# Differential attention: sums of squares by two fp32r passes over a rounded part and a remainder

## Chip, cores and metric

The kernel runs on one core of one Trainium2 chip. The metric is the device time of one execution, in microseconds (us); the time given is the median of three runs.

## What is computed

Two transformer blocks of two layers each over 512 tokens of width 1024. The change lies in the last mixer, differential attention with 8 heads. Cut to what matters:

```python
def rms_norm(x, g):
    return x * lax.rsqrt(jnp.mean(x * x, axis=-1, keepdims=True) + NORM_EPS) * g

k = rms_norm(k.reshape(B, S, 8, 2, 64), k_norm)                 # keys: means over 64 columns
q = rms_norm((xn @ w_q).reshape(B, S, 8, 2, 64), q_gain) * 64 ** -0.5
s = q @ k, causal; p = softmax(s)
a = p[:, :, 0] - lam * p[:, :, 1]                               # two maps per head
o = a @ v                                                       # (S, 128) per head
o = rms_norm(o, head_gain) * (1.0 - lambda_init)                # means over 128 columns
return o.reshape(B, S, 8 * 128) @ w_out
```

So each head needs three sums of squares: of its queries, of its keys and of its output.

## The kernel before

Everything is held transposed, features on the 128 partitions and the 512 tokens along the row (P = 128, TOK = 512). A sum over features is therefore a sum over partitions, and TensorE does it: a matmul with `ones` (all 128 partitions) or `blockones` (two blocks of 64) as its weights.

Large products use fp32r, a form of fp32 of which TensorE reads a rounded value. To keep the precision each operand is split in a high part (an ACT copy that writes fp32r) and a low part (a DVE subtraction, value minus high part), and `mm3` adds three matmuls: high with high, high with low, low with high. Weights come by DMA in chunks of 128 x 2048 into three slots in turn (`raw_w`); `round_weights` makes `high_w` on ACT and `split_weights` makes `low_w` on DVE. The sums of squares, the scores, the transposes and the product with the values are plain fp32 matmuls.

The program is written out by hand, one instruction stream for each engine, each in a fixed order; semaphores alone connect them. Differential attention runs from about 1762 us to 1942 us of the span. `attention_steps` calls `project` for head 0, then `step(p, st, nx, prev)` for p = 0 to 7, then `tail`. In step p the scores of head p are made, while TensorE also computes queries and keys of the next head (`nx`, p + 1), turns the probabilities of the head before (`prev`) and multiplies them by its values, and sums the squares of the output of head p - 2 (`head_sum`). Step 7 has no next head; there the first chunks of the output projection (`resid_first`, `resid_pe`) take that place.

For queries (which = 0) and keys (which = 1) the path is: `half` twice on TensorE (24 matmuls into bank `which`), `raw` on DVE (times `rstd`, into `f_raw`, which is the tile xf), `square` on ACT (into `sq[:, which, :]`), `sums` on TensorE (back into bank `which`), `root` on ACT (Ln, then Exp, into `sq[:, 2 + which, :]`), `normed` on DVE. The next head's `half` may write the bank once Ln has read it (semaphore `logged`). For a head's output: `output` and `output_square` on ACT, `head_sum`, `head_root` on ACT, `head_scale` on DVE, then `rounded` (ACT) and `split` (DVE) for the output projection.

The order on DVE near the end of a step matters to what follows: `norm(p, st)`, `normed(nx, 0)`, `raw(nx, 1)`, `split_weights`, `normed(nx, 1)`. The weights that this `split_weights` finishes are those of the first `half` of the next step. On ACT it is `root(nx, 0)`, `place_values`, `copy_pt`, `round_weights`, `square(nx, 1)`, `output`, `root(nx, 1)`, `output_square`.

Of the kernel before, what the change touches and what calls it, by code (L numbers as in the profile page):

```python
# [31 lines left out]
P = 128  # L32
# [91 lines left out]
def _build(nc, dram, ctx):  # L124
# [43 lines left out]
    def sb(name, shape, dt=F32):  # L168
        return ctx.enter_context(nc.sbuf_tensor(name, shape, dt))

    def sem(name):
        return ctx.enter_context(nc.semaphore(name))
# [4 lines left out]
    sq = sb("sq", [P, 4, TOK])  # L177
# [4 lines left out]
    ones = sb("ones", [P, P])  # L182
    blockones = sb("blockones", [P, P])
    eps = sb("eps", [P, 1])
# [4 lines left out]
    def area(name, specs, start):  # L189

        at, out = start, []
        for n, shape, dt in specs:
            size = int(np.prod(shape[1:])) * 4
            out.append(nc.alloc_sbuf_tensor_at(f"{name}_{n}", list(shape), dt, offset=at))
            at += (size + 63) // 64 * 64
        assert at <= nc.sbuf_usable_end, (name, at, nc.sbuf_usable_end)
        return out, at


    wh, lows = area("high", [(f"w{i}", (P, SLOT), F32R) for i in range(NS)], ring_base)  # L200
# [44 lines left out]
    (f_kh, f_kl, f_vo, f_q0, f_q1, f_k0, f_k1, f_v, f_p, f_pt, f_causal), _ = area("diff", [  # L245
# [3 lines left out]
        ("causal", (P, TOK), F32)], arena_base)  # L249
# [39 lines left out]
    consts_made = sem("consts_made")  # L289
    out_stored = sem("out_stored")  # L290
# [11 lines left out]
    def stand_alone(ins):  # L302


        return ins.wait_op(consts_made, 2, "sem-ge")

# [1583 lines left out]
    F = sems("diff", "v_staged v_placed q_made raw_staged squared sums_made logged rooted q_staged k_staged "  # L1890
             "scored masked exped inverted p_scaled normed turned pt_copied pv_done o_taken")
    H = sems("hn", "squared summed logged rooted scaled rounded split")
# [69 lines left out]
    def diff_pe(pe):  # L1962
# [19 lines left out]
        def sums(p, which):  # L1982

            pe.wait_ge(F["squared"], 2 * p + which + 1)
            pe.wait_ge(F["raw_staged"], 2 * p + which + 1)
            pe.matmul(ps[:, which, :], blockones[:, :], sq[:, which, :], start=True, stop=True)\  # L1986
              .then_inc(F["sums_made"], 1)
# [36 lines left out]
        def head_sum(p):  # L2024

            pe.wait_ge(F["o_taken"], p + 1)
            pe.wait_ge(H["squared"], p + 1)
            pe.matmul(ps[:, O_BANK, :], ones[:, :], sq[:, 0, :], start=True, stop=True)\
              .then_inc(H["summed"], 1)

# [56 lines left out]
    def diff_act(act):  # L2087
        def square(p, which):
            act.wait_ge(F["raw_staged"], 2 * p + which + 1)
            wait_past(act, F["sums_made"], 2 * p - 1 + which)  # L2090
            if which == 0:
                wait_past(act, H["summed"], p - 2)
            act.activation(sq[:, which, :], f_raw[:, which, :], ACT.Square).then_inc(F["squared"], 1)

# [39 lines left out]
        def output_square(p):  # L2134
            act.wait_ge(F["sums_made"], clip(2 * p + 5, 2 * NHD))
            wait_past(act, H["summed"], p)
            act.activation(sq[:, 0, :], ps[:, O_BANK, :], ACT.Square).then_inc(H["squared"], 1)

# [65 lines left out]

        diff_values_act(act, 0)
# [5 lines left out]
    def diff_dve(dve):  # L2211
        def raw(p, which):
            if which == 0:
                dve.wait_ge(F["q_made"], p + 1)
            else:
                dve.wait_ge(w_used, st_diff.base + p + 1)
            wait_past(dve, F["k_staged" if which else "q_staged"], p)
            wait_past(dve, F["squared"], 2 * p - 1 + which)
            dve.tensor_tensor(f_raw[:, which, :], ps[:, which, :], rstd[:, :], ALU.mult)\
               .then_inc(F["raw_staged"], 1)  # L2220

# [50 lines left out]
        def step(p, st, nx, prev):  # L2272
            mask(p, st, (0, 1))
            if nx:
                raw(nx[0], 0)
            else:
                split(2)
            mask(p, st, (2, 3))
            if past_two(p):
                head_scale(p - 2)  # L2280
            if not nx:
                split(3)
            norm(p, st)
            if nx:
                normed(nx[0], nx[1], 0)
                raw(nx[0], 1)
            else:
                split(4)
            if p == NHD - 2:
                split(0, 1)  # L2290
            split_weights(dve, st_diff.base + p + 2)
            if nx:
                normed(nx[0], nx[1], 1)

        def tail(p, st):
            split(5)
            head_scale(p - 1)
            split(6)
            split_weights(dve, st_bout.base + 2)
            head_scale(p)  # L2300
            split(7)

        def project(p, st):
            for which in range(2):
                raw(p, which)
            for which in range(2):
                normed(p, st, which)
# [85 lines left out]
    def _(pe):  # L2393
        pe.wait_ge(consts_made, 2)
        for _ in range(16):
            pe.matmul(ps[:, O_BANK, 0:P], ones[:, :], ones[:, :], start=True, stop=True)
        latents_pe(pe)
# [23 lines left out]
    def _(act):  # L2421
        act.wait_ge(consts_made, 2)
        log_exp(act)
        input_act(act, f_attn0)
# [214 lines left out]
```

## Time and profile before

| | |
|---|---|
| median of three runs | 2322.74 us (2322.34 to 2325.74) |
| profiled execution | span 2323.5 us, first to last instruction; the page gives no other time of it |
| PE (TensorE matmul) busy | 2297.7 us, 99% |
| PEld (weight loads) busy | 1862.3 us, 80% |
| DVE busy | 1115.8 us, 48% |
| ACT busy | 882.1 us, 38% |
| share of PE in the chain that ended last | 94% |
| mean granted TensorE clock | 0.998 of full speed |

The chain that ended last is followed back from the last instruction to what released each step. Where PE has 94% of it, time is PE's own work nearly everywhere, and another engine counts only where PE stood idle for it. A matmul's busy time overlaps the next one's, so what one costs in a row of matmuls is the distance from its start to the next start, not its duration.

### The profile page before, as it was taken

How to read it: one execution, taken by the hardware profiler on the slowest of the kernel's cores; microseconds unless marked ns; L12 is line 12 of the kernel's file. 1: busy time of each engine (PE TensorE's matmuls, PEld its weight loads, DVE VectorE, ACT ScalarE, POOL GpSimd, SP SyncE). 2: the span in 40 equal slices, each digit the busy share in tenths (PEclk: the TensorE clock that was granted, in tenths of full speed). 3: DMA queues.
4: the chain of work that ended last, by engine and by line, in shares of the span. 5: the costliest groups of instructions: out<-in, count | busy, mean ns of one | idle time of the engine just before them, and what ended most of it. 6: DMA issues, size and time to landing. Idle time of an engine off the chain costs nothing.

```text
span 2323.5 us, 26379 instructions
## 1 busy us (share of the span) xinstructions
PE 2297.7 (99%) x10880; PEld 1862.3 (80%) x10880; DVE 1115.8 (48%) x1723; ACT 882.1 (38%) x1399; POOL 0.2 (0%) x4
## 2 busy tenths in 40 slices
PE   9999999999999999999999899999999999999999
PEld 7777888888778888888888788888886667888887
DVE  5655443444575443445577554334444565432432
ACT  5654321223474322224434443223344675421321
POOL 0000000000000000000000000000000000000000
PEclk9999999999999999999999999999999999999999
DMA  3222222322222223223211132322322111222222
GB/s 142 80 82 73 91 98 93 109 85 88 86 97 73 92 91 111 97 80 102 96 64 55 55 109 92 108 91 94 106 98 73 55 55 70 94 91 102 98 91 91
DMA packets 36582, 206.51 MB, mean 89 GB/s; under 512 B 4192, under 2 KB 5088, under 8 KB 17136
## 3 DMA queue, kind: packets, MB, share of 16 engines
q1 hardware_dynamic: 34128, 199.43, 24.9%
q10 hardware_dynamic: 2336, 5.41, 0.7%
q8 instruction: 86, 1.41, 0.3%
q14 instruction: 32, 0.26, 0.0%
HBM read 202.73 MB, written 2.10 MB: 88 GB/s over the span
## 4 chain that ended last, share of the span: by engine, by line
PE 94%; ACT 2%; DVE 2%; issue 1%; ACTq 0%; DVEq 0%
PE ps L309 29%; PE ps L311 28%; PE ps L310 28%; PE ps L1062 2%; PE ps L1649 1%; DVE low_w L335 1%; PE ps L2001 1%; PE ps L1115 1%; PE ps L1086 1%; PE ps L1110 1%; PE ps L1078 0%; ACT high_w L327 0%; PE ps L1674 0%; PE ps L572 0%; PE ps L1986 0%
## 5 line engine op out<-in xcount | busy, mean ns | idle before, releaser
L309 PE MATMUL ps<-xh,high_w 128*128 128x512 f32 x1584 | 628.7, 397 | 0.0
L311 PE MATMUL ps<-xh,low_w 128*128 128x512 f32 x1584 | 617.4, 390 | 0.0
L310 PE MATMUL ps<-xl,high_w 128*128 128x512 f32 x1584 | 616.8, 389 | 0.0
L335 DVE TENSOR_TENSOR low_w<-raw_w,high_w 128x2048 fp32r<-128x2048 f32 (+3 forms) x208 | 422.9, 2034 | 188.2 <-ACT high_w L327 187.9
L327 ACT ACTIVATE high_w<-raw_w 128x2048 fp32r<-128x2048 f32 (+3 forms) x208 | 353.5, 1701 | 288.3 <-PE ps L311 281.4
L309 PEld LDWEIGHTS ps<-xh,high_w 128*128 128x128 f32 x1584 | 297.5, 188 | 64.8 <-issue 5.5
L311 PEld LDWEIGHTS ps<-xh,low_w 128*128 128x128 f32 x1584 | 297.2, 188 | 63.1
L310 PEld LDWEIGHTS ps<-xl,high_w 128*128 128x128 f32 x1584 | 297.7, 188 | 60.5 <-issue 1.4
L309 PE MATMUL ps<-ffn_hidh,high_w 128*128 128x512 f32 x864 | 336.1, 389 | 0.0
L310 PE MATMUL ps<-ffn_hidl,high_w 128*128 128x512 f32 x864 | 336.1, 389 | 0.0
L311 PE MATMUL ps<-ffn_hidh,low_w 128*128 128x512 f32 x864 | 336.1, 389 | 0.0
L700 DVE TENSOR_TENSOR h<-h,ps 128x512 f32<-128x512 f32 (+1 forms) x80 | 63.5, 793 | 328.5 <-PE ps L311 328.5
L311 PEld LDWEIGHTS ps<-ffn_hidh,low_w 128*128 128x128 f32 x864 | 162.2, 188 | 33.8
L309 PEld LDWEIGHTS ps<-ffn_hidh,high_w 128*128 128x128 f32 x864 | 162.2, 188 | 33.7
L310 PEld LDWEIGHTS ps<-ffn_hidl,high_w 128*128 128x128 f32 x864 | 162.2, 188 | 33.6
L748 ACT ACTIVATE sq<-sq 128x512 f32<-128x512 f32 x44 | 27.8, 632 | 334.7 <-DVE sq L772 334.7
L772 DVE TENSOR_TENSOR sq<-ps,rstd 128x512 f32<-128x512 f32 x44 | 30.4, 692 | 216.9 <-PE ps L311 205.9
L756 ACT ACTIVATE sq<-sq 128x512 f32<-128x512 f32 x64 | 39.3, 632 | 208.6 <-DVE sq L788 208.6
L474 ACT ACTIVATE xh<-h,gains 128x512 fp32r<-128x512 f32 x56 | 38.7, 718 | 182.3 <-DVE h L700 179.4
L788 DVE SCALAR_TENSOR_TENSOR sq<-ps,rstd 128x512 f32<-128x512 f32 x64 | 41.2, 686 | 126.5 <-PE ps L311 115.4
L309 PE MATMUL ps<-high_w,xh 128*128 128x256 f32 (+2 forms) x256 | 86.4, 337 | 0.3 <-DVE low_w L335 0.3
L310 PE MATMUL ps<-low_w,xh 128*128 128x256 f32 (+2 forms) x256 | 83.5, 326 | 0.0
(265 smaller groups left out, 2465.5 us busy)
## 6 DMA issues: line engine op xcount, KB each, us to landing
raw_w<-in_w_f_gu SPq DMA_DIRECT2D x44, 1024.0 KB, 4.8
raw_w<-in_w_m_up SPq DMA_DIRECT2D x32, 1024.0 KB, 4.8
raw_w<-in_w_m_dn SPq DMA_DIRECT2D x32, 1024.0 KB, 4.8
raw_w<-in_w_f_dn SPq DMA_DIRECT2D x32, 704.0 KB, 4.0
raw_w<-in_w_b_qk SPq DMA_DIRECT2D x8, 1024.0 KB, 4.8
raw_w<-in_w_e_qk SPq DMA_DIRECT2D x4, 1024.0 KB, 5.2
raw_w<-in_w_e_out SPq DMA_DIRECT2D x4, 1024.0 KB, 5.1
raw_w<-in_w_o_q SPq DMA_DIRECT2D x8, 512.0 KB, 3.6
```

The lines of the kernel that those rows point to most:

```text
L309: pe.matmul(out, sh, mh, start=start, stop=False)
L310: pe.matmul(out, sh, ml, start=False, stop=False)
L311: return pe.matmul(out, sl, mh, start=False, stop=stop)
L327: act.activation(wh[slot][:, 0:elems], raw[slot][:, 0:elems], ACT.Copy).then_inc(w_rounded, 1)
L335: dve.tensor_tensor(wl[slot][:, 0:elems], raw[slot][:, 0:elems], wh[slot][:, 0:elems].bitcast(F32), ALU.subtract).then_inc(w_split, 1)
L474: act.activation(hi[:, t, :], h[:, t, :], ACT.Copy, scale=weight(t)).then_inc(F.s["rounded"].sem, 1)
L700: dve.tensor_tensor(to, to, ps[:, 2 * par:2 * par + R.nt, :], ALU.add).then_inc(R.added.sem, 1)
L748: act.activation(sq[:, par, :], sq[:, par, :], ACT.Silu).then_inc(s["acted"].sem, 1)
L756: act.activation(sq[:, 2 + j, :], sq[:, j, :], ACT.Square).then_inc(s["acted"].sem, 1)
L772: dve.tensor_tensor(sq[:, par, :], ps[:, 2 * par, :], rstd[:, :], ALU.mult)\
L788: dve.scalar_tensor_tensor(out=sq[:, j, :], in0=ps[:, 2 * par + j, :], scalar=0.0, in1=rstd[:, :], op0=ALU.max, op1=ALU.mult)\
L1062: pe.matmul(score_block(A, n), heads_q(A, st, hh, i), heads_k(A, st, hh, i), start=True, stop=True).then_inc(s["scored"].sem, 1)
```

## The change

The squares of queries, keys and outputs are split too. ACT copies the squares into a new tile `f_high` in fp32r, DVE writes squares minus `f_high` over the squares (`sqr` is the same memory as `sq`, seen as fp32r), and TensorE adds two fp32r matmuls, over the high part and over the remainder. Their weights are `ones_r` and `blockones_r`, rounded copies of `ones` and `blockones`, made once on ACT. There is one `f_high` for all, so an ACT copy into it waits until the sums over its last content are done.

```diff
+    def column_sums(pe, out, high, low):
+        pe.matmul(out, ones_r[:, :], high, start=True, stop=False)
+        return pe.matmul(out, ones_r[:, :], low, start=False, stop=True)
...
         def sums(p, which):
-            pe.wait_ge(F["squared"], 2 * p + which + 1)
+            pe.wait_ge(F["sum_low"], 2 * p + which + 1)
             pe.wait_ge(F["raw_staged"], 2 * p + which + 1)
-            pe.matmul(ps[:, which, :], blockones[:, :], sq[:, which, :], start=True, stop=True)\
+            pe.wait_ge(F["blocks_rounded"], 1)
+            pe.matmul(ps[:, which, :], blockones_r[:, :], f_high[:, :], start=True, stop=False)
+            pe.matmul(ps[:, which, :], blockones_r[:, :], sqr[:, which, :], start=False, stop=True)\
               .then_inc(F["sums_made"], 1)
...
         def head_sum(p):
             pe.wait_ge(F["o_taken"], p + 1)
-            pe.wait_ge(H["squared"], p + 1)
-            pe.matmul(ps[:, O_BANK, :], ones[:, :], sq[:, 0, :], start=True, stop=True)\
-              .then_inc(H["summed"], 1)
+            pe.wait_ge(H["sum_low"], p + 1)
+            column_sums(pe, ps[:, O_BANK, :], f_high[:, :], sqr[:, 0, :]).then_inc(H["summed"], 1)
...
         def square(p, which):
             act.wait_ge(F["raw_staged"], 2 * p + which + 1)
-            wait_past(act, F["sums_made"], 2 * p - 1 + which)
+            wait_past(act, F["sums_made"], 2 * p + which)
             if which == 0:
                 wait_past(act, H["summed"], p - 2)
             act.activation(sq[:, which, :], f_raw[:, which, :], ACT.Square).then_inc(F["squared"], 1)
+            act.wait_ge(F["squared"], 2 * p + which + 1)
+            act.activation(f_high[:, :], sq[:, which, :], ACT.Copy).then_inc(F["sum_high"], 1)
...
         def output_square(p):
-            act.wait_ge(F["sums_made"], clip(2 * p + 5, 2 * NHD))
+            act.wait_ge(F["sums_made"], clip(2 * p + 6, 2 * NHD))
             wait_past(act, H["summed"], p)
             act.activation(sq[:, 0, :], ps[:, O_BANK, :], ACT.Square).then_inc(H["squared"], 1)
+            act.wait_ge(H["squared"], p + 1)
+            act.activation(f_high[:, :], sq[:, 0, :], ACT.Copy).then_inc(H["sum_high"], 1)
...
+        def low_part(p, which):
+            dve.wait_ge(F["sum_high"], 2 * p + which + 1)
+            dve.tensor_tensor(sqr[:, which, :], sq[:, which, :], f_high[:, :].bitcast(F32), ALU.subtract)\
+               .then_inc(F["sum_low"], 1)
+
+        def head_low(p):
+            dve.wait_ge(H["sum_high"], p + 1)
+            dve.tensor_tensor(sqr[:, 0, :], sq[:, 0, :], f_high[:, :].bitcast(F32), ALU.subtract)\
+               .then_inc(H["sum_low"], 1)
...
         def step(p, st, nx, prev):
             mask(p, st, (0, 1))
+            if past_two(p):
+                head_low(p - 2)
...
             mask(p, st, (2, 3))
+            if nx:
+                low_part(nx[0], 0)
...
+            if nx:
+                low_part(nx[0], 1)
             split_weights(dve, st_diff.base + p + 2)
...
         def tail(p, st):
+            head_low(p - 1)
             split(5)
             head_scale(p - 1)
             split(6)
             split_weights(dve, st_bout.base + 2)
+            head_low(p)
             head_scale(p)
             split(7)
...
             for which in range(2):
+                low_part(p, which)
                 normed(p, st, which)
...
+        act.activation(ones_r[:, :], ones[:, :], ACT.Copy).then_inc(ones_rounded, 1)
```

Two more lines belong to it: TensorE waits for `ones_rounded` once, behind its sixteen first matmuls on `ones`, and ACT makes `blockones_r` ahead of the copies of the values, where differential attention starts.

The order of the instructions in the fixed streams, at three places. First DVE in `project`, the only head whose queries and keys are not made inside a step; `xf` is written by `raw`, `diff_q` and `diff_k` by `normed`. Before:

```order
L2219 TENSOR_TENSOR xf<-ps,rstd 128x512 [waits diff_q_made]
L2219 TENSOR_TENSOR xf<-ps,rstd 128x512 [waits w_used]
L2225 SCALAR_TENSOR_TENSOR diff_q_128<-xf,gains,sq 128x512 [waits diff_rooted]
L2225 SCALAR_TENSOR_TENSOR diff_k_130<-xf,gains,sq 128x512 [waits diff_rooted]
L2239 ISA diff_p,small<-ps,diff_causal 128x128 [waits diff_scored,consts_made]
```

And after the change (`parts_sq` is `sqr`, `squares_sq` is `sq`, `diff_high` is `f_high`):

```order
L2236 TENSOR_TENSOR xf<-ps,rstd 128x512 [waits diff_q_made]
L2236 TENSOR_TENSOR xf<-ps,rstd 128x512 [waits w_used]
L2241 TENSOR_TENSOR parts_sq<-squares_sq,diff_high 128x512 [waits diff_sum_high]
L2252 SCALAR_TENSOR_TENSOR diff_q_130<-xf,gains,squares_sq 128x512 [waits diff_rooted]
L2241 TENSOR_TENSOR parts_sq<-squares_sq,diff_high 128x512 [waits diff_sum_high]
L2252 SCALAR_TENSOR_TENSOR diff_k_132<-xf,gains,squares_sq 128x512 [waits diff_rooted]
```

The subtraction for the queries stands behind `raw` of the keys, and the one for the keys behind `normed` of the queries. ACT's stream at the same place, after the change:

```order
L2104 ACTIVATE squares_sq<-xf 128x512 [waits diff_raw_staged]
L2106 ACTIVATE diff_high<-squares_sq 128x512 [waits diff_squared]
L2104 ACTIVATE squares_sq<-xf 128x512 [waits diff_sums_made,diff_raw_staged]
L2106 ACTIVATE diff_high<-squares_sq 128x512 [waits diff_squared]
L2114 ACTIVATE squares_sq<-ps,eps 128x512 [waits diff_sums_made]
L2117 ACTIVATE squares_sq<-squares_sq 128x512 [waits diff_logged]
```

The square of the keys now waits for a sum, that of the queries, and both squares and copies stand ahead of the first Ln.

Second, DVE at the end of step 0, as of every step that has a next head. Before:

```order
L2225 SCALAR_TENSOR_TENSOR diff_q_129<-xf,gains,sq 128x512 [waits diff_rooted]
L2219 TENSOR_TENSOR xf<-ps,rstd 128x512 [waits diff_squared,diff_k_staged,w_used]
L335 TENSOR_TENSOR low_w_55<-raw_w_52,high_w_49 128x2048 [waits w_rounded]
L2225 SCALAR_TENSOR_TENSOR diff_k_131<-xf,gains,sq 128x512 [waits diff_rooted]
L2239 ISA diff_p,small<-ps,diff_causal 128x128 [waits diff_normed,diff_scored,diff_exped,consts_made]
```

And after the change:

```order
L2252 SCALAR_TENSOR_TENSOR diff_q_131<-xf,gains,squares_sq 128x512 [waits diff_rooted]
L2236 TENSOR_TENSOR xf<-ps,rstd 128x512 [waits diff_squared,diff_k_staged,w_used]
L2241 TENSOR_TENSOR parts_sq<-squares_sq,diff_high 128x512 [waits diff_sum_high]
L345 TENSOR_TENSOR low_w_57<-raw_w_54,high_w_51 128x2048 [waits w_rounded]
L2252 SCALAR_TENSOR_TENSOR diff_k_133<-xf,gains,squares_sq 128x512 [waits diff_rooted]
```

The subtraction for the keys stands between `raw` and the splitting of the next weights, and it waits for an ACT copy.

Third, DVE in `tail`. Before, from `split(5)` on (`diff_kl` is written by `split`, `diff_vo` by `head_scale`):

```order
L2269 TENSOR_TENSOR diff_kl<-diff_vo,diff_kh 128x512 [waits hn_rounded]
L2263 SCALAR_TENSOR_TENSOR diff_vo<-diff_vo,small,sq 128x512 [waits hn_squared,hn_rooted]
L2269 TENSOR_TENSOR diff_kl<-diff_vo,diff_kh 128x512 [waits hn_rounded]
L335 TENSOR_TENSOR low_w_57<-raw_w_54,high_w_51 128x2048 [waits w_rounded]
L2263 SCALAR_TENSOR_TENSOR diff_vo<-diff_vo,small,sq 128x512 [waits hn_squared,hn_rooted]
L2269 TENSOR_TENSOR diff_kl<-diff_vo,diff_kh 128x512 [waits hn_rounded]
```

And after the change:

```order
L2246 TENSOR_TENSOR parts_sq<-squares_sq,diff_high 128x512 [waits hn_sum_high]
L2296 TENSOR_TENSOR diff_kl<-diff_vo,diff_kh 128x512 [waits hn_rounded]
L2290 SCALAR_TENSOR_TENSOR diff_vo<-diff_vo,small,squares_sq 128x512 [waits hn_squared,hn_rooted]
L2296 TENSOR_TENSOR diff_kl<-diff_vo,diff_kh 128x512 [waits hn_rounded]
L345 TENSOR_TENSOR low_w_59<-raw_w_56,high_w_53 128x2048 [waits w_rounded]
L2246 TENSOR_TENSOR parts_sq<-squares_sq,diff_high 128x512 [waits hn_sum_high]
L2290 SCALAR_TENSOR_TENSOR diff_vo<-diff_vo,small,squares_sq 128x512 [waits hn_squared,hn_rooted]
L2296 TENSOR_TENSOR diff_kl<-diff_vo,diff_kh 128x512 [waits hn_rounded]
```

The subtraction for the last head stands behind the splitting of the third chunk of the output weights.

## Rows read from the trace of the kernel before

**Rows 1.** The page: the span, and each engine's busy time.

```profile
span 2323.5 us, 26379 instructions
PE 2297.7 (99%) x10880; PEld 1862.3 (80%) x10880; DVE 1115.8 (48%) x1723; ACT 882.1 (38%) x1399; POOL 0.2 (0%) x4
```

**Rows 2.** Single lines: duration in ns (min/median/max), first and last start, shape.

```profile
L1986 PE MATMUL ps<-sq,blockones x32: 591/592/697, 1767.1 to 1910.3; 128*128 128x512 f32 x32
L2028 PE MATMUL ps<-sq,ones x16: 591/592/595, 1814.1 to 1938.0; 128*128 128x512 f32 x16
L2269 DVE TENSOR_TENSOR diff_kl<-diff_vo,diff_kh x8: 682/692/693, 1907.8 to 1941.7; 128x512 fp32r<-128x512 f32 x8
L2152 ACT ACTIVATE diff_kh<-diff_vo x8: 613/626/631, 1906.3 to 1941.0; 128x512 fp32r<-128x512 f32 x8
```

**Rows 3.** Timeline of PE in step 1: start us, us, engine, line [idle before].

```profile
1799.20 0.39 PE L311 MATMUL ps<-xh,low_w 128*128 128x512 f32 x1
1799.43 1.02 PE L1986 MATMUL ps<-sq,blockones 128*128 128x512 f32 x2
1800.29 0.93 PE L2011 MATMUL ps<-ident,diff_p 128*128 128x128 f32 x7
```

**Rows 4.** Timeline of step 2, start of step 3: DVE, ACT and PE.

```profile
1807.41 0.50 PE L309 MATMUL ps<-diff_kh,high_w 128*128 128x512 f32 x1 [0.41 <-DVE low_w L335]
...
1814.31 0.69 DVE L2219 TENSOR_TENSOR xf<-ps,rstd 128x512 f32<-128x512 f32 x1 [1.96 <-PE ps L311]
1815.25 0.63 ACT L2093 ACTIVATE sq<-xf 128x512 f32<-128x512 f32 x1 [1.89 <-PE ps L2028]
1817.02 0.60 ACT L2112 ACTIVATE diff_p<-diff_p,small 128x384 f32<-128x384 f32 x1
1819.76 0.20 DVE L2247 RECIPROCAL small<-small 128x8 f32<-128x8 f32 x1 [0.59 <-ACT diff_p L2112]
1824.67 0.69 DVE L2219 TENSOR_TENSOR xf<-ps,rstd 128x512 f32<-128x512 f32 x1 [0.75 <-PE ps L311]
1825.71 2.29 DVE L335 TENSOR_TENSOR low_w<-raw_w,high_w 128x2048 fp32r<-128x2048 f32 x1 [0.35 <-ACT high_w L327]
1828.06 0.50 PE L309 MATMUL ps<-diff_kh,high_w 128*128 128x512 f32 x1 [0.41 <-DVE low_w L335]
```

**Rows 5.** Timeline of the end of `project`.

```profile
1767.26 0.69 DVE L2219 TENSOR_TENSOR xf<-ps,rstd 128x512 f32<-128x512 f32 x1 [3.72 <-PE ps L311]
...
1769.86 0.40 PE L310 MATMUL ps<-diff_kl,high_w 128*128 128x512 f32 x1
```

**Rows 6.** Timeline of the end of step 0: DVE and PE.

```profile
1784.79 0.68 DVE L2219 TENSOR_TENSOR xf<-ps,rstd 128x512 f32<-128x512 f32 x1
...
1787.72 0.50 PE L309 MATMUL ps<-diff_kh,high_w 128*128 128x512 f32 x1 [0.41 <-DVE low_w L335]
```

**Rows 7.** Timeline of the end of step 6: ACT and PE.

```profile
1909.11 0.62 ACT L2093 ACTIVATE sq<-xf 128x512 f32<-128x512 f32 x1
...
1911.69 0.50 PE L309 MATMUL ps<-diff_kh,high_w 128*128 128x512 f32 x1 [0.78 <-ACT sq L2101]
```

**Rows 8.** Timeline of `tail`: PE, ACT, DVE.

```profile
1931.17 0.50 PE L309 MATMUL ps<-diff_kh,high_w 128*128 128x512 f32 x1 [1.07 <-DVE diff_kl L2269]
...
1935.56 0.59 ACT L2137 ACTIVATE sq<-ps 128x512 f32<-128x512 f32 x1
...
1937.57 1.02 PE L2028 MATMUL ps<-sq,ones 128*128 128x512 f32 x2
...
1937.99 2.29 DVE L335 TENSOR_TENSOR low_w<-raw_w,high_w 128x2048 fp32r<-128x2048 f32 x1 [4.12 <-ACT high_w L327]
```

**Rows 9.** By stretch: us, busy PE, PEld, DVE, ACT, POOL; then granted clock, DMA.

```profile
1308.00:1311.00 3.00, 0.50 (x3) 0.06 (x1) 3.00 (x5) 0.93 (x3) 0.00 (x0) 1.00 0.00 0
1311.00:1314.00 3.00, 2.73 (x11) 2.56 (x12) 3.00 (x7) 1.60 (x4) 0.00 (x0) 0.53 0.00 0
...
1769.50:1787.70 18.20, 16.26 (x69) 10.55 (x67) 12.59 (x32) 10.98 (x25) 0.00 (x0) 1.00 0.22 79
```

More of the change, by code:

```diff
@@ L176, in _build @@
     xl = sb("xl", [P, KD, TOK], F32R)
-    sq = sb("sq", [P, 4, TOK])
     rstd = sb("rstd", [P, TOK])
@@ L182, in _build @@
     ones = sb("ones", [P, P])
+    ones_r = sb("ones_r", [P, P], F32R)
     blockones = sb("blockones", [P, P])
+    blockones_r = sb("blockones_r", [P, P], F32R)
     eps = sb("eps", [P, 1])
@@ L197, in area @@
         return out, at
-    wh, lows = area("high", [(f"w{i}", (P, SLOT), F32R) for i in range(NS)], ring_base)
+    (sq,), _ = area("squares", [("sq", (P, 4, TOK), F32)], ring_base)
+    (sqr,), highs = area("parts", [("sq", (P, 4, TOK), F32R)], ring_base)
+    wh, lows = area("high", [(f"w{i}", (P, SLOT), F32R) for i in range(NS)], highs)
     raw, arena_base = area("raw", [(f"w{i}", (P, SLOT), F32) for i in range(NS)], lows)
@@ L244, in _build @@
     g_z, g_wg, g_reset = g_e0[0:16, :], g_tmp0[0:16, :], g_e1
-    (f_kh, f_kl, f_vo, f_q0, f_q1, f_k0, f_k1, f_v, f_p, f_pt, f_causal), _ = area("diff", [
+    (f_kh, f_kl, f_vo, f_q0, f_q1, f_k0, f_k1, f_v, f_p, f_pt, f_causal, f_high), _ = area("diff", [
         ("kh", (P, KD, TOK), F32R), ("kl", (P, KD, TOK), F32R), ("vo", (P, KD, TOK), F32),
@@ L248, in _build @@
         ("v", (P, TOK), F32), ("p", (P, 3, CAUSAL_AT[-1]), F32), ("pt", (P, TB, TOK), F32),
-        ("causal", (P, TOK), F32)], arena_base)
+        ("causal", (P, TOK), F32), ("high", (P, TOK), F32R)], arena_base)
     f_raw, f_lam = xf, f_p[:, 2, 0:256]
@@ L289, in _build @@
     consts_made = sem("consts_made")
+    ones_rounded = sem("ones_rounded")
     out_stored = sem("out_stored")
@@ L1889, in _build @@
     L = sems("lam", "loaded dots exped made")
-    F = sems("diff", "v_staged v_placed q_made raw_staged squared sums_made logged rooted q_staged k_staged "
+    F = sems("diff", "blocks_rounded sum_high sum_low v_staged v_placed q_made raw_staged squared sums_made logged rooted q_staged k_staged "
              "scored masked exped inverted p_scaled normed turned pt_copied pv_done o_taken")
-    H = sems("hn", "squared summed logged rooted scaled rounded split")
+    H = sems("hn", "sum_high sum_low squared summed logged rooted scaled rounded split")
     NHD = 8
@@ L2203, in project @@
                 root(p, which)
+        act.wait_ge(const_loaded, 64)
+        act.activation(blockones_r[:, :], blockones[:, :], ACT.Copy).then_inc(F["blocks_rounded"], 1)
         diff_values_act(act, 0)
@@ L2396, in _ @@
             pe.matmul(ps[:, O_BANK, 0:P], ones[:, :], ones[:, :], start=True, stop=True)
+        pe.wait_ge(ones_rounded, 1)
         latents_pe(pe)
```

## The prediction

> **What bounds the kernel now.** I read the page first: PE is busy 2297.7 us of a span of 2323.5 us [rows 1], so 26 us at most are waits. Then I read differential attention engine by engine in the timeline, and asked where PE stands idle and for whom. The reader is to see one pattern. Inside a step PE is never idle. At the end of a step it is: its first matmul of the next step comes 0.41 us late and was released by `low_w`, the DVE splitting of the weights; that splitting started at 1825.71, 0.35 us after DVE was free, because the ACT rounding `high_w` came last [rows 4]. So the work of the step is PE's, and its end is set by a short chain on DVE and ACT. There is no slack at that point: what is put into DVE's stream ahead of `low_w` moves the next step.
>
> **What the change removes.** A sum of squares is one fp32 matmul, recorded as two of 592 ns; 32 records on `blockones` and 16 on `ones` are 24 sums [rows 2]. What one costs in a running stream is the distance of starts: 1799.43 to 1800.29, so 0.86 us, while an fp32r matmul takes 0.23 us, from 1799.20 to 1799.43 [rows 3]. Two of them are 0.46 us, so 0.40 us are saved for each sum, and 24 x 0.40 = 9.6 us of PE work go away. That alone would be the gain if nothing else came later.
>
> **What it adds.** 24 ACT copies and 24 DVE subtractions, 128x512. The trace has the same two shapes in `rounded` and `split`: 0.63 us and 0.69 us [rows 2]. A copy that waits for ACT's own square starts when the square ends, 0.63 + 0.03 = 0.66 us behind its start. The next DVE instruction starts some 0.08 us before the end of a subtraction of this size, so one holds DVE's stream for 0.61 us. For the handover between engines I take 0.03 us, and 0.06 us into PE; rows 4 show the latter (1825.71 + 2.29 = 1828.00, PE at 1828.06). The two copies of constants cost nothing: `ones_r` is made while ACT waits for the first input, and `blockones_r` lies in a long ACT idle before the copies of the values. Without that cover each would be one small ACT instruction, some 0.3 us.
>
> **Project, +4.4 us.** All times here are of the clock of the trace before. `raw` of the keys runs from 1767.26 to 1767.95 [rows 5]. The first subtraction stands behind it, so it runs 1767.87 to 1768.56 and the query sum starts at 1768.62, 0.57 us of PE with the restart. Its result comes at 1769.35, and only now may ACT square the keys (one `f_high`): square 1769.39, copy 1770.05, then the Ln and Exp of the queries, 1770.58 and 1771.30 to 1771.93. DVE's `normed` of the queries stands ahead of the key subtraction: 1771.97, then the subtraction 1772.64 to 1773.33, and the key sum starts at 1773.39 and gives way at 1773.96. Before, that was at 1769.52 (the start of L310 at 1769.86, less 0.34 for the first matmul after an idle stretch) [rows 5]. The difference is 4.4 us. It was one sum waiting for one square; it becomes a chain of ten instructions over three engines.
>
> **Step 0, +2.4 us.** PE saves 0.40 us at the query sum. But the copy of the queries delays the exponentials by 0.36 us and with them `norm` on DVE, and DVE has no gap there: `raw` of the keys started right behind it, at 1784.79, without idle [rows 6]. With the 4.4 us it starts at 1784.79 + 4.4 + 0.36 = 1789.55. Then raw 0.69, square and copy (0.03 + 0.66 + 0.62), subtraction behind 0.03 us and 0.61 us to the next start, splitting 2.29, and 0.06: 1794.54. PE started at 1787.72 [rows 6], so the whole shift is 6.8 us and 2.4 of it is new.
>
> **Step 1, +1.4 us.** The same reckoning from where the query sum is 0.40 us earlier and bounds the ACT chain: 1808.79 for 1807.41 [rows 4].
>
> **Steps 2 to 5, +1.3 us each, +5.1 us.** The head sum and the query sum save 0.80 us before the critical end. On the other side: `raw` of the queries ends at 1815.00 [rows 4], the square starts at 1815.03, the copy at 1815.69, the two of `head_root` behind it, and the exponentials start at 1817.48 where they started at 1817.02. So `norm` comes 0.46 us late (1819.76), and DVE, which had 0.75 us idle before `raw` at 1824.67, can start it at 1824.38 at best; PE would allow 1823.87. From 1824.35: square 1825.07, copy 1825.73, end 1826.35, subtraction 1826.38, splitting 1826.99 to 1829.28, PE 1829.34, against 1828.06. What is late is the splitting; queued behind it are `normed` of the keys and the next masks, and they have time, since the scores come 3 us later.
>
> **Step 6, +1.1 us; step 7, -0.1 us.** Step 6 also rounds and splits two heads' outputs ahead of the weights, so ACT squares only at 1909.11 [rows 7]; 0.6 us earlier by the savings, then copy, subtraction and splitting end at 1912.69 and PE goes at 1912.75 for 1911.69. Step 7 has one head sum and one subtraction on DVE just ahead of it, which nearly cancel.
>
> **Tail, +4.5 us.** The copy for head 6 stands ahead of the transposed probabilities, and the wait of PE for `split(5)`, at 1931.17 [rows 8], grows by 0.66 us. From there the square of head 7 starts at 1936.22, its copy at 1936.88, `high_w` runs 1937.41 to 1939.33, `low_w` 1939.36 to 1941.65, and only behind it the subtraction, to 1942.26. The head sum goes at 1942.32; it was at 1937.57, before `low_w` at 1937.99 was even under way [rows 8]. It now waits for the splitting of weights with which it has nothing to do: 4.75 us, less 0.29 saved in the sum itself, is 4.5 us.
>
> The sum: 4.4 + 2.4 + 1.4 + 5.1 + 1.1 - 0.1 + 4.5 = 18.8 us. The 9.6 us saved are in it already.
>
> **The clock.** In the gated-attention stage PE worked 0.50 us of the three from 1308 to 1311 and came back at a granted clock of 0.53 for the next 3 us, the lower level of 1.2 GHz, where 1.00 is 2.4 GHz [rows 9]. At that level 3 us do the work of 1.6, so one such fall costs some 1.5 us, 1.6 with the edge. By my reckoning PE is idle nearly as long or longer at three places: between the two sums of `project` (4.0 us), at the end of step 0 (3.8 us and 1.6 us with one sum between), and in `tail` (4.1 us). I add 3 x 1.6 = 4.8 us. Bounds: none, if the clock holds through them, and 9 x 1.9 = 17 us if every step end costs one as well; I take three because the stretch of rows 9 was idle for 2.5 of 3 us and the other step ends have 0.9 and 1.6 us with a sum between.
>
> The Trainium skill says in "TensorE: Matmul & The Clock Gate", section "What's actually happening", that the throttled state is the default and activity releases it, so that idle stretches are paid for twice. The trace agrees by the 0.53 of that stretch. Without the rule and the row the sum stays at 18.8 us; with it, 23.6 us.
>
> **Forecast.** 18.8 + 4.8 = 23.6 us more. The profiled execution spans 2323.5 us, 0.8 above the median of 2322.74; I add to the median: 2346.3 us, 1.0% slower.
>
> **The rivals.**
> 1. The clock holds, or falls once: 18.8 to 20.4 us, 2341.5 to 2343 us. Against it stands the 0.53; for it, that the two idle stretches at step ends here are short. Chance 0.15.
> 2. The clock falls at the ends of most steps too, and stays low longer than 3 us: 30 to 36 us, 2353 to 2359 us. For it: with 0.9 and 1.6 us idle around one sum, PE does little for over 3 us there, six times more. Against: step 0 has 1.9 us of idle, nearly all at its end, and the clock stays at 1.00 [rows 9]. Chance 0.2.
> 3. The step ends are hidden: the subtraction is done by the time the weights are rounded, so steps 0 to 7 gain 0.40 us for each of some 21 sums, 8.4 us, and `project` and `tail` lose 8.9 us. 2323 us, no change. It needs `square` to come before `high_w` on ACT, but it stands behind it in ACT's fixed order. Chance 0.05.
> 4. Faster: as 3, and the waits in `project` and `tail` are shorter than one saving each, so that the 9.6 us stay, 2313 us. The one mechanism is that PE alone bounds the stage. It decides at the step end: the chain from `raw` to PE may grow by no more than the 0.80 us that PE gains ahead of it, and I reckon 2.08 us. For it stands only the 99% of the page. Chance 0.03.
> 5. The change doesn't do what it says: a pass over `f_high` costs as much as half an fp32 sum, 0.43 us. Then nothing is saved and the result is some 9 us later than forecast on the sums ahead of the critical points, 2355 us. Against it: 0.23 us for all fp32r matmuls of this shape. Chance 0.02.
>
> The forecast itself has 0.55, with a range of its own of 2343 to 2351 us: each of the seven boundaries may be off by 0.3 us, and each fall of the clock may last from 3 to 5 us and so cost 1.4 to 2.5 us. The range with 8 in 10 reaches down into rival 1 and up into rival 2: 2338 to 2358 us. Slower by over 0.2%, which is 4.6 us and about what a measurement of this kernel can tell from no change: 0.55 + 0.15 + 0.2 + 0.02 = 0.92. Within: 0.05. Faster: 0.03.
>
> **What would show it.** In the trace after: L1997 and L1998 start 0.23 us apart; PE idle of about 4 us before the second sum of `project`, and 3.8 us at the end of step 0; six steps of 21.9 us where they took 20.65; each with `low_w` starting some 1.3 us later and a DVE wait for `diff_high` ahead of it; about 4 us idle before the last head sum, released by DVE L2246; a clock below 1 behind these. Wrong it is if PE's step end is still released at the old distance from the query sum, or if DVE runs the subtraction with no wait in front.

## The result and the profile after

The changed kernel takes 2356.89 us (median of four runs, 2353.8 to 2358.18) where the one before took 2324.24 us (four runs, 2322.34 to 2325.92). The ratio is 1.0143, 95% interval 1.0132 to 1.0155: 32.7 us slower. The forecast was 2346.3 us, in a range of 2338 to 2358. The profiled execution spans 2354.2 us and took 2355.97 us, so a span is some 2 us less than the time of the same execution.

The page of the changed kernel, its answer to [rows 1], with the head of the chain that ended last:

```profile
span 2354.2 us, 26430 instructions
PE 2303.6 (98%) x10880; PEld 1869.5 (79%) x10880; DVE 1130.1 (48%) x1747; ACT 897.4 (38%) x1425; POOL 0.2 (0%) x4
...
PE 91%; ACT 4%; DVE 3%; issue 2%; DMA 0%; SPq 0%; ACTq 0%; DVEq 0%
```

PE's share of the chain fell from 94% to 91%, and ACT and DVE have more of it; there are 24 more instructions on DVE and 26 on ACT, two of these for the rounded constants. PE's busy time even rose, by 6 us, though by the prediction's reckoning 9.6 us of work were taken away: matmuls at half clock are longer. The view of what PE waited for (total us, times, longest) names the new waits:

```profile
PE ps L1997 <- DVE parts_sq L2241: 14.9, 9, 4.1
PE ps L319 <- DVE low_w L345: 9.1, 7, 1.5
...
PE ps L314 <- DVE parts_sq L2246: 4.0, 1, 4.0
PE ps L319 <- DVE diff_kl L2296: 1.7, 2, 1.2
PE ps L319 <- ACT squares_sq L2114: 1.5, 1, 1.5
```

L2241 and L2246 are the subtractions for queries and keys and for head outputs; they were not there before. `low_w` cost PE 2.8 us in seven waits before and costs 9.1 now.

The end of `project` in the timeline (start us, us, engine, line, and in brackets the idle time before and its releaser), the answer to [rows 5]; before, PE was idle there once, for 0.59 us:

```profile
1764.24 0.69 DVE L2236 TENSOR_TENSOR xf<-ps,rstd 128x512 f32<-128x512 f32 x1 [3.72 <-PE ps L321]
1764.85 0.68 DVE L2241 TENSOR_TENSOR parts_sq<-squares_sq,diff_high 128x512 fp32r<-128x512 f32 x1
...
1765.59 0.51 PE L1997 MATMUL ps<-diff_high,blockones_r 128*128 128x512 f32 x1 [1.38 <-DVE parts_sq L2241]
...
1766.42 0.63 ACT L2104 ACTIVATE squares_sq<-xf 128x512 f32<-128x512 f32 x1 [4.57 <-PE ps L1998]
1767.08 0.63 ACT L2106 ACTIVATE diff_high<-squares_sq 128x512 fp32r<-128x512 f32 x1
1767.62 0.67 ACT L2114 ACTIVATE squares_sq<-ps,eps 128x512 f32<-128x512 f32 x1
...
1769.65 0.68 DVE L2241 TENSOR_TENSOR parts_sq<-squares_sq,diff_high 128x512 fp32r<-128x512 f32 x1
...
1770.39 0.79 PE L1997 MATMUL ps<-diff_high,blockones_r 128*128 128x512 f32 x1 [4.07 <-DVE parts_sq L2241]
1770.98 0.63 PE L1998 MATMUL ps<-parts_sq,blockones_r 128*128 128x512 f32 x1
1771.41 0.63 PE L319 MATMUL ps<-diff_kh,high_w 128*128 128x512 f32 x1
```

From `raw` of the keys to their sum it is 6.15 us, where the forecast reckoned 6.13. The last two lines show what the idle stretch did besides: each takes 0.63 us, and they start 0.43 us apart and not 0.23, which is the lower clock.

The end of step 4, with DVE's order as [rows 4] showed it for step 2, and PE:

```profile
1883.02 0.69 DVE L2236 TENSOR_TENSOR xf<-ps,rstd 128x512 f32<-128x512 f32 x1
1885.06 0.69 DVE L2241 TENSOR_TENSOR parts_sq<-squares_sq,diff_high 128x512 fp32r<-128x512 f32 x1 [1.36 <-ACT diff_high L2106]
1885.67 2.29 DVE L345 TENSOR_TENSOR low_w<-raw_w,high_w 128x2048 fp32r<-128x2048 f32 x1
...
1885.81 0.51 PE L1997 MATMUL ps<-diff_high,blockones_r 128*128 128x512 f32 x1 [0.76 <-DVE parts_sq L2241]
...
1888.01 0.50 PE L319 MATMUL ps<-diff_kh,high_w 128*128 128x512 f32 x1 [1.46 <-DVE low_w L345]
```

`raw` follows DVE's work without idle, so DVE and not PE sets its start. Then DVE stands 1.36 us waiting for the ACT copy, with the ready splitting of the weights behind it. PE is idle twice, 0.76 and 1.46 us.

The tail, the answer to [rows 8]:

```profile
1960.84 0.59 ACT L2150 ACTIVATE squares_sq<-ps 128x512 f32<-128x512 f32 x1
1961.46 0.63 ACT L2152 ACTIVATE diff_high<-squares_sq 128x512 fp32r<-128x512 f32 x1
...
1963.93 2.29 DVE L345 TENSOR_TENSOR low_w<-raw_w,high_w 128x2048 fp32r<-128x2048 f32 x1 [4.79 <-ACT high_w L337]
1966.14 0.69 DVE L2246 TENSOR_TENSOR parts_sq<-squares_sq,diff_high 128x512 fp32r<-128x512 f32 x1
...
1966.97 0.47 PE L314 MATMUL ps<-diff_high,ones_r 128*128 128x512 f32 x1 [3.96 <-DVE parts_sq L2246]
```

The squares are there at 1961.4, but the subtraction waits behind the splitting of a weight chunk, and PE is idle 3.96 us.

The granted clock by stretch (columns: stretch, its length, busy PE, PEld, DVE, ACT, POOL with their counts, clock, DMA share, GB/s): the wait in `project` and what follows it, a step without and one with a fall of the clock, and the whole stage:

```profile
1766.00:1770.40 4.40, 0.34 (x3) 0.01 (x1) 1.35 (x2) 2.46 (x4) 0.00 (x0) 0.92 0.50 210
1770.40:1776.30 5.90, 5.90 (x14) 4.45 (x14) 0.75 (x1) 1.32 (x2) 0.00 (x0) 0.50 0.01 3
...
1842.70:1864.60 21.90, 19.38 (x89) 13.51 (x89) 14.43 (x36) 16.07 (x36) 0.00 (x0) 1.00 0.15 49
1864.60:1888.00 23.40, 20.95 (x88) 14.60 (x88) 14.37 (x36) 16.01 (x36) 0.00 (x0) 0.93 0.13 46
...
1765.00:1975.00 210.00, 177.40 (x730) 123.76 (x731) 121.79 (x287) 133.79 (x287) 0.00 (x0) 0.91 0.12 41
```

Before, the stage ran at 1.00 throughout. Now it has a mean of 0.91. The clock goes to its lower level, 0.50, seven times: behind the waits of `project` and `tail` and at the ends of steps 0, 1, 3, 5 and 6. Below, a fall means such a stretch at the lower clock. Two steps with the same instructions take 21.9 us without a fall and 23.4 us with one.

### The profile page after: what moved, and what is told of

It reads as the page before. It is cut to its first block, busy times and chain, and to the rows that moved or that the text cites. A ratio compares the mean times of both kernels' runs of the same rounds, so it can differ in the third digit from the quotient of the medians.

```text
span 2354.2 us, 26430 instructions
## 1 busy us (share of the span) xinstructions
PE 2303.6 (98%) x10880; PEld 1869.5 (79%) x10880; DVE 1130.1 (48%) x1747; ACT 897.4 (38%) x1425; POOL 0.2 (0%) x4
## 4 chain that ended last, share of the span: by engine, by line
PE 91%; ACT 4%; DVE 3%; issue 2%; DMA 0%; SPq 0%; ACTq 0%; DVEq 0%
PE ps L319 28%; PE ps L321 28%; PE ps L320 28%; PE ps L1072 2%; PE ps L1659 1%; DVE low_w L345 1%; PE ps L1125 1%; ACT high_w L337 1%; PE ps L1096 1%; PE ps L1120 1%; ACT diff_p L2125 1%; PE ps L2013 0%; PE ps L1088 0%; ACT diff_pt L2132 0%; ACT squares_sq L2104 0%
## 5 line engine op out<-in xcount | busy, mean ns | idle before, releaser
L758 ACT ACTIVATE squares_sq<-squares_sq 128x512 f32<-128x512 f32 x44 | 27.8, 633 | 334.6 <-DVE squares_sq L782 334.6
L782 DVE TENSOR_TENSOR squares_sq<-ps,rstd 128x512 f32<-128x512 f32 x44 | 30.4, 692 | 216.8 <-PE ps L321 205.8
L766 ACT ACTIVATE squares_sq<-squares_sq 128x512 f32<-128x512 f32 x64 | 39.4, 633 | 208.6 <-DVE squares_sq L798 208.6
L798 DVE SCALAR_TENSOR_TENSOR squares_sq<-ps,rstd 128x512 f32<-128x512 f32 x64 | 41.2, 686 | 126.4 <-PE ps L321 115.4
L321 PE MATMUL ps<-high_w,xl 128*128 128x256 f32 (+2 forms) x256 | 83.0, 324 | 0.0
```

The costliest lines, as they stand in the source:

```text
L321: return pe.matmul(out, sl, mh, start=False, stop=stop)
L758: act.activation(sq[:, par, :], sq[:, par, :], ACT.Silu).then_inc(s["acted"].sem, 1)
L766: act.activation(sq[:, 2 + j, :], sq[:, j, :], ACT.Square).then_inc(s["acted"].sem, 1)
L782: dve.tensor_tensor(sq[:, par, :], ps[:, 2 * par, :], rstd[:, :], ALU.mult)\
L798: dve.scalar_tensor_tensor(out=sq[:, j, :], in0=ps[:, 2 * par + j, :], scalar=0.0, in1=rstd[:, :], op0=ALU.max, op1=ALU.mult)\
```

## The experiments

My theory was that two costs add up: serial chains of square, copy and subtraction ahead of waits of PE, in `project`, at the step ends and in `tail` (18.8 us), and falls of the clock behind the idle stretches (the rest). Rivals: the waits alone, each added instruction alike, or passes that save nothing. Differences below are between the medians of a kernel and of the kernel before in the same set of runs; step lengths are distances between the first scores of two steps in the timeline.

**e1_fill: keep PE busy where it waits.**

```diff
+        def fill(bank, n):
+            for _ in range(n):
+                pe.matmul(ps[:, bank, :], ones_r[:, :], xh[:, 0, :], start=True, stop=True)
...
             if nx:
+                pe.wait_ge(F["logged"], 2 * nx[0] + 1)
+                fill(0, {0: 13, 6: 5}.get(p, 2))
                 sums(nx[0], 1)
+                fill(0, 5)
```

The same filling stands ahead of both sums of `project` (4 and 14) and ahead of the last head sum (14).

> The changed kernel (32.7 us over the one before) with TensorE kept busy by matmuls that nobody reads (weights ones_r, moving xh) where it stands idle in differential attention: 4 and 14 of them ahead of the two sums of project, 13 in step 0, 5 in step 6 and 2 elsewhere ahead of the key sums, 5 behind each key sum, 14 ahead of the last head sum; at 0.23 us each they fit in the idle stretches. Theory (a serial chain worth 18.8 us, and falls of the clock that cost the other 14): the granted clock stays at 1.00 in the stage and the time is 18 to 22 us over the kernel before; the waits stay where they are. Rival 1 (the waits and the added instructions alone cost the 32.7 us, the low clock only fills time in which PE would wait anyway): no change, 31 to 34 us over. Rival 2 (the filling delays the sums): over 34.

2344.14 us for 2324.15, 20.0 us over, ratio 1.0085 (1.0071 to 1.0099). The whole stage of this kernel, by stretch:

```profile
1765.00:1965.00 200.00, 188.25 (x846) 133.18 (x845) 122.63 (x289) 133.64 (x287) 0.00 (x0) 1.00 0.13 43
```

The end of step 2 in its timeline (L2044 is the filling):

```profile
1833.88 0.70 PE L2044 MATMUL ps<-xh,ones_r 128*128 128x512 f32 x2
1834.91 0.51 PE L1997 MATMUL ps<-diff_high,blockones_r 128*128 128x512 f32 x1 [0.33 <-DVE parts_sq L2250]
1835.25 0.40 PE L1998 MATMUL ps<-parts_sq,blockones_r 128*128 128x512 f32 x1
1835.48 1.32 PE L2044 MATMUL ps<-xh,ones_r 128*128 128x512 f32 x5
1837.11 0.50 PE L319 MATMUL ps<-diff_kh,high_w 128*128 128x512 f32 x1 [0.31 <-DVE low_w L345]
```

The waits stand where they did, released by the same instructions; what is left of them, 0.33 and 0.31 us here, is the part that the filling does not cover. From key sum to next step it is 2.20 us as in the changed kernel. Apart from the filling only the clock differs, at 1.00. More work, and 12.7 us less time (32.7 less 20.0): the falls of the clock are shown, and so is their price. Rival 1 is out. Four steps take 21.83, 21.83, 21.82 and 21.82 us here.

**e2_tail: one DVE instruction earlier.**

```diff
-            split_weights(dve, st_bout.base + 2)
             head_low(p)
+            split_weights(dve, st_bout.base + 2)
             head_scale(p)
```

> The changed kernel with one DVE instruction moved in tail: the subtraction for head 7 stands ahead of the splitting of the third chunk of the output weights and not behind it. Theory: the last head sum no longer waits for that splitting, the 3.96 us of idle ahead of it go, and the fall of the clock behind them with it (1.5 to 2.4 us): 26 to 28 us over the kernel before instead of 32.7. Rival 1 (the idle there is paid back later in the projection, whose own waits are shorter): 31 to 33. Rival 2 (the splitting that is now 0.7 us later delays the third chunk): over 28, with an idle of PE released by low_w behind the second chunk.

2348.03 us, 23.9 us over, ratio 1.0098 (1.0083 to 1.0114). The direction is right and the size is 2 us past the expectation. The wait is gone entirely (PE timeline):

```profile
1960.42 0.39 PE L321 MATMUL ps<-diff_kh,low_w 128*128 128x512 f32 x1
1960.76 0.47 PE L314 MATMUL ps<-diff_high,ones_r 128*128 128x512 f32 x1
```

Its 3.96 us and one fall at 1.8 us explain some 6 us of the 8.8. The rest lies in how long the clock stays low. The stage by stretch, the changed kernel first and then this one:

```profile
1765.00:1985.00 220.00, 187.40 (x774) 132.04 (x775) 127.53 (x294) 138.12 (x293) 0.00 (x0) 0.91 0.14 48
```

```profile
1765.00:1985.00 220.00, 191.20 (x809) 135.45 (x810) 132.71 (x299) 140.42 (x295) 0.00 (x0) 0.94 0.15 49
```

The profile has six falls (behind `project` and the ends of steps 0, 3, 4, 5 and 6) for the other's seven. Summed over half-microsecond stretches the clock is low for 27.3 us here and for 37.6 us there. At the price that e1_fill gives, 12.7 us for those 37.6, the 10.2 us less are worth some 3.5 us, and 7.4 of the 8.8 us are accounted for; each side is one execution, and the number and length of falls vary. That the order costs at least the 4 us is shown.

**e3_keys: key sums by one fp32 matmul again.** `square`, `low_part` and `sums` skip the copy, the subtraction and the second pass where `which` is 1:

```diff
+            if which:
+                pe.wait_ge(F["squared"], 2 * p + 2)
+                pe.wait_ge(F["raw_staged"], 2 * p + 2)
+                pe.matmul(ps[:, which, :], blockones[:, :], sq[:, which, :], start=True, stop=True)\
+                  .then_inc(F["sums_made"], 1)
+                return
```

> The changed kernel with the key sums undone: keys' squares are summed by one fp32 matmul again, with no copy and no subtraction, in project and in all steps; query and head sums keep the two passes. Theory (the cost is where the chain stands ahead of the next weights, and in project, where the keys waited for the one high-part tile): step ends are released as early as before or 0.6 us earlier, project costs 0.5, and only the tail's 4.5 us and its clock fall stay: 2 to 5 us over the kernel before. Rival (each added copy, subtraction and pass costs alike, wherever it stands): keys are 8 of 24 sums, so a third of 32.7 us goes, 21 to 23 us over.

2327.26 us, 3.1 us over, ratio 1.0015 (1.0006 to 1.0024). Undoing a third of the change takes away nine tenths of its cost; the rival, 21 to 23 us, is out. The profile has one fall left in the stage, behind the wait in `tail`. PE at the end of step 3:

```profile
1845.52 1.02 PE L1997 MATMUL ps<-squares_sq,blockones 128*128 128x512 f32 x2
1846.81 0.50 PE L319 MATMUL ps<-diff_kh,high_w 128*128 128x512 f32 x1 [0.26 <-DVE low_w L345]
```

The step end waits 0.26 us for `low_w`, where it was 0.41 before the change, and the steps take 19.97 us for 20.61: query and head sums do save, 0.64 us a step.

**e4_mix: e2_tail and e3_keys together.**

> Both edits: key sums by one fp32 matmul again, and the last subtraction ahead of the splitting in tail. Theory: by the same reckoning project +0.5, step 0 +0.4, step 1 -0.4, steps 2 to 5 -0.6 each, step 6 -0.5, step 7 -0.1, tail +0.4, so 2 us under the kernel before (1 to 4 under). Rival (the step ends have another bound, the rounding on ACT behind the added copies): 0 to 3 over.

2322.81 us for 2324.15, 1.3 us under, ratio 0.9992 (0.9983 to 1.0001): inside the expectation, but not told from no change. Its profile shows what holds it back, at the end of step 0, where the delayed exponentials delay `raw` of the keys:

```profile
1782.39 1.12 PE L1997 MATMUL ps<-squares_sq,blockones 128*128 128x512 f32 x2 [2.33 <-ACT squares_sq L2110]
1783.92 0.62 PE L319 MATMUL ps<-diff_kh,high_w 128*128 128x512 f32 x1 [0.41 <-DVE low_w L345]
```

The wait was 1.55 us before the change and is 2.33 here, and in this execution the clock fell behind it. In e3_keys, which has the same instructions there and a wait of 2.32 us, it did not. So step 0 took 20.13 us here and 18.53 there.

**e5_heads: two passes for head outputs alone, with the order of e2_tail.** Queries and keys are summed as before the change.

> Only the head outputs' sums keep the two passes, and the last subtraction stands ahead of the splitting in tail; query and key sums are one fp32 matmul as in the kernel before. Theory: the copy and the subtraction of a head output lie in idle stretches of ACT and DVE, each of the head sums inside a step gives its 0.40 us (six of them), tail costs 0.4: 1.5 us under the kernel before (0 to 3 under). Rival (an added instruction on ACT at the end of a step delays the next exponentials): 0 to 3 over.

2321.09 us for 2323.37, 2.3 us under, ratio 0.9991 (0.9982 to 1.0). Steps 2 to 5 take 20.22 to 20.28 us where they took 20.61 to 20.66: a head sum gives 0.33 to 0.44 us, and 0.40 was expected. The interval just reaches no change, so it is by these steps that the rival is out.

**e6_fill_fp32: the price of the passes.** The sums of e1_fill as one fp32 matmul over the high part.

```diff
-            pe.matmul(ps[:, which, :], blockones_r[:, :], f_high[:, :], start=True, stop=False)
-            pe.matmul(ps[:, which, :], blockones_r[:, :], sqr[:, which, :], start=False, stop=True)\
+            pe.matmul(ps[:, which, :], blockones[:, :], f_high[:, :].bitcast(F32), start=True, stop=True)\
```

> The kernel with the filling matmuls (e1_fill, measured 20.0 us over the one before), and every sum as one fp32 matmul over the high part instead of two fp32r passes; it leaves out the remainder, which is still made and waited for, so only the price of the passes on TensorE changes. Theory: 0.40 us come back at each sum in a running stream (7 query sums and 6 head sums in the steps), some 0.3 at the two of project and the last, and nothing at the key sums of the steps, behind which PE waits for the weights: 26 us over the kernel before (25 to 28). Rival 1 (the passes save nothing that counts): 19 to 21 over. Rival 2 (all 24 count alike): 29 to 30 over.

2345.31 us for 2323.37, 21.9 us over, ratio 1.0095 (1.0081 to 1.0109): 1.9 us over e1_fill, where I expected 6. The intervals of the two overlap, so I read it in the timelines. Steps 2 to 5 take 22.40 us and not 21.83, 0.57 us more, and from the first scores of step 0 to those of step 7 it is 153.7 us for 150.4. So the saving is real, but my 0.80 us a step were too much. The line of `raw` of the keys in e1_fill (first) and in this kernel points at the reason:

```profile
1832.12 0.68 DVE L2245 TENSOR_TENSOR xf<-ps,rstd 128x512 f32<-128x512 f32 x1
```

```profile
1851.17 0.69 DVE L2245 TENSOR_TENSOR xf<-ps,rstd 128x512 f32<-128x512 f32 x1
```

Neither has idle before it. DVE sets that start in both, so what PE saves arrives there only as far as it moved DVE's own inputs. This is my reading of the lines; no run isolates it.

**e7_order: the weights ahead of the key subtraction.**

```diff
+            split_weights(dve, st_diff.base + p + 2)
             if nx:
                 low_part(nx[0], 1)
-            split_weights(dve, st_diff.base + p + 2)
```

> The changed kernel with one pair swapped on DVE at the end of each step: the splitting of the next weights stands ahead of the key subtraction. Theory: the splitting starts when the rounding is done, and the subtraction and the key sum come behind it, so PE starts the next step some 0.7 us earlier in five or six steps and 1.1 in step 0, but no more, because the key sum still stands ahead of the next half in PE's stream: 27 to 30 us over the kernel before, depending on the falls of the clock (the one long idle stretch of 2 us in place of two). Rival (the splitting alone set the step end): 2 us less for each of seven steps, 17 to 20 us over.

2346.0 us for 2323.37, 22.6 us over, ratio 1.0091 (1.0076 to 1.0106): between the two expectations, and both missed. PE at the end of step 3:

```profile
1860.04 0.51 PE L1997 MATMUL ps<-diff_high,blockones_r 128*128 128x512 f32 x1 [1.72 <-DVE parts_sq L2241]
1860.38 0.40 PE L1998 MATMUL ps<-parts_sq,blockones_r 128*128 128x512 f32 x1
1860.61 0.40 PE L319 MATMUL ps<-diff_kh,high_w 128*128 128x512 f32 x1
```

The mechanism is the theory's: a step without a fall takes 21.03 us for 21.83, 0.8 us less. What I had not reckoned is that in this profile one idle stretch of 1.72 us (1.90 at step 1) and no second one leaves the clock at 1.00: none of steps 1 to 5 ends in a fall here, while three of them did in the changed kernel. Four falls are left, behind `project` (idle for 4.07 us), the ends of step 0 (4.46 us) and of step 6 (2.77 and 0.78 us), and `tail` (3.96 us). Of the 10.1 us that this order takes off the 32.7, three falls fewer at 1.8 us are 5.4; the chain of the steps gives 4.6, as e9_all shows below.

**e8_late: two passes only where they are covered.** e4_mix, with the queries of heads 0 and 1 by one matmul too.

> Two passes only where they are hidden: head sums, and query sums from head 2 on; keys, and the queries of heads 0 and 1 (whose sums have no cover in project and step 0), are summed by one fp32 matmul; the last subtraction stands ahead of the splitting in tail. Theory: project and step 0 are as in the kernel before and without the fall of the clock that the other mixed kernel had in step 0; step 1 gives 0.4, steps 2 to 5 give 0.64 each as measured there, step 6 0.5, tail costs 0.4: 3 us under the kernel before (2 to 4.5 under). Rival (what the sums save is lost again behind the stage): within 1 of it.

2320.32 us for 2323.16, 2.8 us under, ratio 0.9986 (0.9977 to 0.9995). It has the lowest ratio of all versions, 0.14% under the kernel before; the interval leaves out no change, narrowly, and does not tell it from e5_heads. Step 0 is back at 18.17 us and step 2 at 19.96.

**e9_all: all sums by two passes, with the three remedies** of e1_fill, e2_tail and e7_order, the filling in the steps before the key sum alone, and none before the last head sum.

> All 24 sums by two passes as in the changed kernel, with its three remedies at once: the splitting of the weights ahead of the key subtraction, the last head's subtraction ahead of the splitting in tail, and matmuls that nobody reads in the idle stretches (4 and 14 in project, 16 in step 0, 9 in step 6, 6 in the other steps). Theory (chain and clock add up, and the three parts of the chain are separate): project 4.4, steps 4, tail 0.4, clock 0: 8 to 11 us over the kernel before. Rival (the remedies overlap, so that less is left to gain once the clock holds): 13 or more over.

2333.19 us for 2323.16, 10.0 us over, ratio 1.0043 (1.003 to 1.0057), as the sum of the parts had it. The clock's mean is 0.999. From the first scores of step 0 to those of step 7 it is 145.8 us for 140.8, so 5 us are left in the steps, 4.6 less than the 150.4 us of e1_fill; the largest single part is `project`, whose chain no remedy shortens.

## Why the prediction was right, and where it was off

The measured time is 10.6 us above the forecast of 2346.3: 1.5 us because the kernel before now has a median of 2324.24 and not 2322.74, 1.2 us in the chain, and 7.9 us in the clock. The mechanism was right and the result lies in the range of 2338 to 2358 us. But the forecast's own range, 2343 to 2351 us, missed it; the wider one holds it, 1.1 us below its end, only because it reached up into rival 2.

- **What bounds the stage** was right: `low_w` at the step ends, and no slack there.
- **The pass prices** were right: L1997 to L1998 start 0.23 us apart in a running stream, the restart 0.34.
- **Project, +4.4 us**: from `raw` of the keys to their sum 6.15 us, reckoned 6.13. From that `raw` to the first scores it is 9.57 us in e1_fill and was 5.23, so +4.3.
- **The steps**: in e1_fill, where the clock holds, step 0 takes 20.59 us for 18.20, +2.4 (forecast 2.4); step 1 21.04 for 19.70, +1.3 (1.4); steps 2 to 5 +1.2 each, 4.8 in all (5.1); step 6 21.43 for 20.38, +1.05 (1.1). The sign "six steps of 21.9 us where they took 20.65" was miscounted: only steps 2 to 5 took that, and those four take 21.8.
- **Tail, +4.5 us**: an idle of 3.96 us, reckoned 4.1. From the first scores of step 7 to the end of the span it is 414.4 us in e1_fill for 410.2, +4.2 (4.4 with step 7).
- **The chain as a whole, 18.8 us**: e1_fill measured 20.0 (medians, about 3 us of uncertainty). The profiled executions of it and of the kernel before have the clock low for as long upstream, 10.2 us each, and their spans differ by 17.9 us.
- **The clock, 4.8 us, was mis-sized.** I counted three falls at 1.6 us. There were seven, and the clock accounts for 12.7 us, 1.8 us each. The number is the larger error: I took the other step ends to be safe because their idle stretches, 0.9 and 1.6 us, were shorter than the stretch of [rows 9]. Four of those six fell all the same, steps 1, 3 and 5 with 0.8 to 0.9 and 1.5 us of idle around one sum, and step 6 with 1.7 and 1.5 us. The size was low too: the clock stayed at its lower level for 3.4 to 6.8 us, where I had reckoned with 3 in the sum and 3 to 5 in the range. The Trainium skill ("TensorE: Matmul & The Clock Gate", "What's actually happening") has the throttled state as the default, which activity releases. The seven falls, each at an idle stretch of TensorE, agree with that; which of the like step ends fall is not explained by it, nor by a run here.
- **Rival 2 came true**, with its chance of 0.2: the clock fell at the ends of most steps, five of seven, and stayed low longer than 3 us, for 30 to 36 us in all, where 32.7 were measured. The rival had named the reason, two idle stretches around one sum, and I had set step 0 of the kernel before against it: 1.9 us of idle and no fall. Like step ends fell in three cases of five, so one that does not fall could not decide it.
- **The base**: I added to the median, with the note that the span was 0.8 us above it. A span is 2 us below the time of its own execution, so that execution was one of the longer ones. It had two falls of the clock upstream of the change, in the gated attention, 10.2 us of low clock. The profiled execution of the changed kernel has 3.4 us there: the wait of 2.78 us behind which the clock fell before came without a fall. This fits the stage's start, 3 us earlier in the trace after, and the spans' difference of 30.7 us beside 32.7 of the medians.
- **Rivals 1, 3, 4 and 5** are out: a clock that holds or falls once (seven falls), a chain hidden at the step ends (the waits of PE for the key sum and `low_w` there), a stage bound by PE alone, and passes as dear as half an fp32 sum (0.23 us start to start).

## What to carry to other kernels

A matmul made cheaper by splitting its operand trades time on the busiest engine for latency on two others; what counts is where in the chain the sum stands. The same edit gave 0.14% where its copy and subtraction had cover, and cost 1.4% when it was also made where they stood ahead of work that others waited for. So go through an in-order stream and ask of each inserted instruction what is queued behind it: here it was the splitting of weights, twice, once with the inserted instruction ahead of it and once behind. And an idle stretch of TensorE is to be priced with its clock: here two short ones around one sum cost a fall at three of five step ends, and one of 1.7 us at none of five.

## What the runs showed that I had not expected

- The clock fell at three of five step ends whose instructions and idle stretches (0.8 to 0.9 and 1.47 us, one sum between) are the same, and not at the other two; in e2_tail it was three of the same five again, partly others. A step with a fall takes 23.3 to 23.8 us from first scores to first scores, where it takes 21.0 to 21.8 without, 1.5 to 2.8 us more.
- A single idle stretch of 1.72 to 1.90 us (e7_order) left the clock at 1.00 at all of these step ends. One of 2.3 us left it at 1.00 in one profile (e3_keys) and not in another (e4_mix).
- Matmuls that nobody reads, 95 of them in the idle stretches, made the kernel 12.7 us faster.
- The eleven profiled executions begin this stage up to 5.7 us apart, and the clock upstream is low in them for 3.4 to 10.2 us; a step's length, read between two marks of the timeline, is the better measure of a change in it.
